# High parts of the weights by a converting DMA instead of staging buffer and ScalarE, and a sixth slot per piece

## The reference

```
layer 1:  nx = rmsnorm(h);  proj = nx @ w_in            # 1024 x 3088
          gated linear attention and dilated attention over proj -> mixed
          h += mixed @ w_out
          h += square(relu(rmsnorm(h) @ w_ff1)) @ w_ff2 # 1024 x 4096, 4096 x 1024
          final rmsnorm
layer 2:  xn = rms_norm(h); proj = xn @ w_in_2          # 1024 x 5632
          stick-breaking attention, HGRN2 recurrence over proj
          mixed = sigmoid(gate_sb) * (o_sb @ w_branch[:512]) + sigmoid(gate_hg) * (o_hg @ w_branch[512:])
          h += mixed @ w_out_2
          h += (silu(hn @ w_gate) * (hn @ w_up)) @ w_down   # inner width 2816
```

## Time and profile before

| | us |
|---|---|
| median of three runs | 1414.1 |
| the profiled execution | 1414.06 |
| its span, first to last instruction | 1412.4 |
| PE busy | 1386.7 (98%) |
| ACT busy | 865.4 (61%) |
| DVE busy | 624.8 (44%) |
| POOL busy | 192.7 (14%) |

### The profile page before, as it was taken

One profiled execution on the slowest core, in us unless ns is written; L12 is line 12 of the kernel. 1 busy time (PEld: TensorE's weight loads), 2 busy tenths in 40 slices (PEclk: granted clock), 3 DMA queues, 4 the chain that ended last, 5 costly groups with the idle time before them and its releaser, 6 DMA issues.

```text
span 1412.4 us, 17525 instructions
## 1 busy us (share of the span) xinstructions
PE 1386.7 (98%) x6784; PEld 1119.7 (79%) x6784; DVE 624.8 (44%) x1216; ACT 865.4 (61%) x1272; POOL 192.7 (14%) x227
## 2 busy tenths in 40 slices
PE   9999999999999999999989999999999999999999
PEld 6977966788888888887867768787788888888887
DVE  6055365521211212357578779954534422341232
ACT  5574566654544535666678778776557645663561
POOL 0210000111111111111100001011111111111110
PEclk9999999999999999999999999999999999999999
DMA  7975544698888888877745556679988888888975
GB/s 227 248 167 131 143 117 97 151 208 194 189 196 196 194 189 199 189 166 170 169 100 119 120 119 163 169 172 269 221 198 186 192 192 200 192 192 194 197 164 125
DMA packets 72791, 248.00 MB, mean 176 GB/s; under 512 B 8098, under 2 KB 8114, under 8 KB 72580
## 3 DMA queue, kind: packets, MB, share of 16 engines
q0 software_dynamic: 31536, 113.54, 47.0%
q1 hardware_dynamic: 40452, 131.73, 28.9%
q10 hardware_dynamic: 720, 1.61, 0.3%
HBM read 240.52 MB, written 6.32 MB: 175 GB/s over the span
## 4 chain that ended last, share of the span: by engine, by line
PE 78%; ACT 8%; DVE 8%; issue 3%; DMA 2%; SPq 0%; DVEq 0%; ACTq 0%
PE bank L466 24%; PE bank L470 24%; PE bank L473 24%; ACT WH L770 2%; ACT WL L778 1%; PE bank L581 1%; PE bank L600 1%; DVE eb L1416 1%; DMA RAW<-in_w_out 1%; PE bank L624 1%; PE bank L614 1%; ACT eb L924 1%; ACT hs L720 1%; DMA gates<-hs 1%; DVE eb L1412 0%
## 5 line engine op out<-in xcount | busy, mean ns | idle before, releaser
L466 PE MATMUL bank<-NH,WH 128*128 128x512 f32 x1152 | 466.4, 406 | 3.5 <-ACT NH L875 1.7
L470 PE MATMUL bank<-NL,WH 128*128 128x512 f32 x1152 | 449.2, 391 | 1.0 <-DVE NL L1160 0.5
L473 PE MATMUL bank<-NH,WL 128*128 128x512 f32 x1152 | 449.3, 391 | 0.0
L770 ACT ACTIVATE WH<-RAW 128x1024 fp32r<-128x1024 f32 (+2 forms) x227 | 235.2, 1037 | 204.8 <-PE bank L473 191.5
L466 PEld LDWEIGHTS bank<-NH,WH 128*128 128x128 f32 x1152 | 216.9, 188 | 69.0 <-issue 26.3
L470 PEld LDWEIGHTS bank<-NL,WH 128*128 128x128 f32 x1152 | 217.0, 188 | 47.8 <-issue 3.8
L473 PEld LDWEIGHTS bank<-NH,WL 128*128 128x128 f32 x1152 | 216.8, 188 | 46.2
L778 ACT ACTIVATE WL<-WH 128x1024 fp32r<-128x1024 f32 (+2 forms) x219 | 229.5, 1048 | 5.6
L470 PE MATMUL bank<-AL,WH 128*128 128x512 f32 x432 | 168.2, 389 | 0.0
L466 PE MATMUL bank<-AH,WH 128*128 128x512 f32 x432 | 168.1, 389 | 0.0
L473 PE MATMUL bank<-AH,WL 128*128 128x512 f32 x432 | 168.0, 389 | 0.0
(11 more groups left out here) (288 smaller groups left out, 1637.7 us busy)
## 6 DMA issues: line engine op xcount, KB each, us to landing
RAW<-in_w_in SPq DMA_DIRECT2D x64, 512.0 KB, 5.5
RAW<-in_w_ff SPq DMA_DIRECT2D x64, 512.0 KB, 6.2
WL<-in_w_ff POOLq DMA_DIRECT2D x64, 512.0 KB, 8.7
WL<-in_w_in POOLq DMA_DIRECT2D x62, 512.0 KB, 7.8
RAW<-in_w_gu SPq DMA_DIRECT2D x44, 512.0 KB, 6.6
WL<-in_w_gu POOLq DMA_DIRECT2D x44, 512.0 KB, 8.8
RAW<-in_w_down SPq DMA_DIRECT2D x20, 512.0 KB, 5.1
WL<-in_w_down POOLq DMA_DIRECT2D x20, 512.0 KB, 8.7
```

The lines of the kernel that those rows point to most:

```text
L466: e.matmul(o, a[0], a[1], start=(k == 0), stop=False)
L470: e.matmul(o, b[0], b[1], start=False, stop=False)
L473: mm = e.matmul(o, c[0], c[1], start=False, stop=(k == t.kt - 1))
L770: e.activation(WH[p % HL][:, 0:n], RAW[p % RAWS][:, 0:n], ACT.Copy).then_inc(*act.sig("high", p))
```

## The change

The RAW buffers and the rounding on ACT stay for the first eight pieces only (RAW now lies where temporaries of a later stage lie). From the ninth piece on POOL issues a DMA that reads float32 from HBM and writes float32r into WH itself (`highs`). It waits, as ACT did, for the last matmul with the slot's former piece. ACT then negates WH into WL, and the adding DMA follows as before. HL is 6 instead of 5. Due times move: the negation is ordered 8.5 instead of 1.5 behind the slot's coming free, the adding DMA 10 instead of 3. SP no longer issues weights after the eighth piece. PE waits for the landing of WH where it waited for ACT.

```diff
-HL = 5
+HL = 6
...
-        RAW = [sb(f"RAW{i}", PIECE) for i in range(RAWS)]
...
         temps = top[0]
+        RAW = [sb(f"RAW{i}", PIECE) for i in range(RAWS)]
+        top[0] = temps
...
-        ADDED = 8
+        ADDED, NEGATED = 8, 8.5
...
+        def high(p):
+
+
+            return ("high" if p < ADDED else f"high_loaded{p % HL}", p)
...
-            if p < 5:
-                return [-20.0, -18.4, -15.4, -13.4, -11.5][p]
+            if p < HL:
+                return [-20.0, -18.4, -15.4, -13.4, -11.5, 4.1][p]
             return plan.used[p - HL] + 0.1

         def low_time(p):
-            return split_time(p) + (3.0 if p >= ADDED else 0.05)
+            return split_time(p) + (NEGATED + 1.5 if p >= ADDED else 0.05)
...
-                        pe.wait_ge(("high", p), hi(x, k0 + k))
+                        pe.wait_ge(high(p), hi(x, k0 + k))
...
             def splits():
-                for p, (u, k, m) in enumerate(plan.pieces):
+                for p, (u, k, m) in enumerate(plan.pieces[:ADDED]):
...
-                        yield split_time(p) + 1.5
+                        yield split_time(p) + NEGATED
                         n = m * plan.units[u][4]
-                        act.wait_ge(("high", p))
+                        act.wait_ge(high(p))
...
+            def highs():
+                for p, (u, k, m) in enumerate(plan.pieces):
+                    if p < ADDED:
+                        continue
+                    yield split_time(p)
+                    st, name, i, kt, cols, k0 = plan.units[u]
+                    src = A[name] if i is None else A[name][i]
+                    u0, j0, m0 = plan.pieces[p - HL]
+                    pool.wait_ge(("product", "block", u0, j0 + m0 - 1))
+                    e.dma_start(WH[p % HL][:, 0:m * cols], src[:, k * cols:(k + m) * cols]).then_inc(
+                        *pool.sig(f"high_loaded{p % HL}", p, by=16))
...
-            yield from merge(zeros(), lows(), masks())
+            yield from merge(zeros(), highs(), lows(), masks())
...
             def weights():
-                for p, (u, k, m) in enumerate(plan.pieces):
+                for p, (u, k, m) in enumerate(plan.pieces[:ADDED]):
```

More of the change, by code:

```diff
@@ L1783, in weights @@
                     if p >= RAWS:
-                        sp.wait_ge(low(p - RAWS) if p - RAWS < ADDED else ("high", p - RAWS))
+                        sp.wait_ge(low(p - RAWS))
                     e.dma_start(RAW[p % RAWS][:, 0:m * cols], src[:, k * cols:(k + m) * cols]).then_inc(
```

## The result

The changed kernel takes 1486.6 us (median of four runs, 1484.1 to 1490.4) against 1414.6 us, a ratio of 1.0514 with a 95% interval of 1.0485 to 1.0542: it is slower, by 72 us, where 56 were forecast.

What follows compares the result with a forecast made beforehand. TensorE was taken to bound the kernel, busy 1386.7 of 1412.4 us. The terms −5.1 − 1 + 58 + 3 = +55 us gave 1470 us; the range for 8 in 10 was 1407 to 1590.

Steps and rivals of the forecast that it cites:

- The circle: Dense stages: loads wait behind adding DMAs, these for negations, these for loads; 11.9 us per unit against TensorE's 10.88, +58 us.
- First adding DMA: First link of the circle: an adding DMA issued into an idle queue lands after 5.8 us, as in quiet.
- The second: Link of the circle: the second adding DMA, behind the first in the queue, takes 2.96 us.
- The rest: Last link of the circle: negation, ACT's start and POOL's issue of the next adding DMA, 1.46 us.
- The order of a queue: Queue q0: assumed to serve its DMAs in order of issue, so loads stand behind adding DMAs; no separate size.
- rival 1: Dense stages: the circle does not bind, only gains and the start's cost remain; 1406 to 1414 us, chance 0.27.
- Rival 3: ACT, held at the negation until the load lands, delivers operand rows late; alone 1415 to 1420 us, chance 0.05.
- The half clock: TensorE's granted clock may fall, beyond the sum, if low parts are late by more than 3 us at once.
- wT and the stretch behind it: Attention: TensorE's waits for ACT's copies into wT shorten as roundings leave ACT, −5.1 us.
- The boundaries: Two stage boundaries: the rounding ahead of the operand rows goes, −1 us.
- The start: Program start: pieces 10 and 12 late without the early load into RAW; +3 us, ends 0 and +7.
- Rival 2: Dense stages: the converting load costs 2.96 us like the adding DMA, 13.2 us per unit; 1564 us, chance 0.16.

Runs made afterwards that it cites:

- pool_later: Changed kernel with only POOL's order moved: each adding DMA due 13.5 instead of 10 cells after its slot comes free; 1408.0 us, ratio 0.9962.
- half_adding: Changed kernel with each adding DMA from the ninth piece on carrying only 64 of the 128 partitions, orders untouched; 1395.3 us, ratio 0.987.
- half_columns: Changed kernel with each converting load from the 21st piece on carrying half of the columns on all 128 partitions; 1435.5 us, ratio 1.0153.
- act_later: Changed kernel with ACT's negations due 12 instead of 8.5 cells after the slot, POOL's order nearly kept; 1492.2 us, ratio 1.0559.
- five_slots: Changed kernel with HL 5 again instead of 6, the rest unchanged; 1483.5 us, ratio 1.0486.

## Why the prediction was right

*The sign and the cause: right.* The circle was forecast at 11.9 us and is 12.1. pool_later takes it away and gains 78.6 us, half_adding shortens it and gains 91, half_columns shortens it by 0.85 us and gains 51, act_later leaves it closed and gains nothing.

*Its terms.* First adding DMA 5.8, measured 5.92: the quiet landing was the right choice, since q1 is silent. The second 2.96, measured 3.41: the term that was too small, taken from q0's share with another queue beside it. The converting load 1.68, measured 1.40. The rest 1.46, measured 1.38. With 1.22 us over TensorE's pace, 74 × 1.22 − 17 = +73 us instead of +58; by stages +30.6 and +44.0 = +74.6 were measured. Against the forecast's +55 the dense blocks are 16.6 us dearer, the boundary at qS 8.0 and the start 2.4, and the attention and recurrence give 8.9 more: 18 us in the sum, where without the last they would be 27. So the total came nearer than its parts by some luck.

*The order of a queue: right.* It was an assumption. The landings at 402.7, 405.7 and 407.1 are in the order of issue. The Trainium skill, *DMA: Bandwidth & Descriptors*, "Queues, rings and completion order", has each engine take a queue's descriptors in ring order; the trace agrees.

*One queue instead of two: free.* pool_later keeps everything in q0 and fills the window of 352 us. The same page, "Issuing engines are not separate DMA queues", says that spreading DMAs over issuing engines saves only issue time, and the trace agrees; but the page's rule led to rival 1's time, and that was wrong: bandwidth was free while the order of issue was not.

*Where it shows: wrong.* I expected "PE <- DMA WL" all through f1 and f2, and a difference of 1 us a unit. Only 4.2 us stand there. ACT, held at the negation, delivers AH late instead (34 us in ten waits), mostly at the first unit of a round of f2 or dn. POOL's turns are 12.1 us long as forecast, TensorE's units are not: they take 10.9 us and now and then 19 to 21. The whole stretch from f1 to qS grew from 351.7 to 382.3 us, where I had said about 380. Rival 3 had this mechanism and I said it decided nothing: right for the time, as five_slots shows, and wrong for the rows to look for.

*The half clock.* I had it as a possible addition beyond the sum. It came, mean clock 0.975 against 0.996 (the place before that matters is that of the earlier trace rows), but five_slots with 0.991 takes nearly the same time. That in a loop that sets the pace TensorE's slower stretches use up waiting that was there anyway is my reading of these two runs, not tested by itself.

*wT and the stretch behind it.* Forecast 8.2 to about 3 us; measured 2.0 in three waits, longest 0.8, and the clock behind it stays at 1.00. The whole stretch from kS to br0 gains 14.0 us where I had 5.1: mis-sized. Every kernel without the roundings gains there, 8 to 14 us. That I counted one kind of wait of TensorE and left ACT's lighter load for all the others is the likely reason; no run separates it.

*The boundaries: wrong sign.* −1 us was forecast. Where f1 begins 2.4 us are gained. But in qS, where I had the circle recover at no cost, the rows NH come late and 7.0 us are lost, part of it at half clock (0.57 in 656 to 664 us):

```profile
PE bank L472 <- ACT NH L939: 3.0, 2, 2.7
```

Between br0 and gu 5.7 us go (a part of the last block's 44.0), and TensorE's waits for AH at the turn from f1 to f2 and from gu to dn are where much of the circle is paid.

*The start: near in size, wrong in place.* +3 forecast, +5.4 at f1. Pieces 10 and 12 were not late (the stages up to qD start 0.3 us earlier). Three adding DMAs and two loads, issued between 55 and 60 us, took up to 11 us to land, ACT waited 9.4 us, VectorE's gX was late, and TensorE lost 6.9 us at 97 us, part of it at half clock.

*Rival 2: wrong.* The converting load costs 1.40 us behind other DMAs, not 2.96.

## What to carry to other kernels

When a change makes an engine that issues DMAs wait, write down who waits for whom until the list comes back to its start, sum the links, and compare with the pace of the engine that bounds: if the loop is longer, the difference is paid on every turn, however idle every engine and queue looks. Then move one issue past another before giving up the change: here the same instructions, 5.5 cells later on two engines, turn +5.1% into −1.0%. Check such a shift at the start of the program too, where slots come free in another rhythm.

## What the runs showed of the hardware

- A converting DMA into a rounded type costs about what a plain one does: 0.18 us a packet of 4 KB, and 1.40 us of the queue for 512 KB, against 1.68 for a plain load with another queue beside it. Issued at 20.5 us of the changed kernel, one landed after 4.1 us, against 3.6 for a plain load in quiet.
- A load onto 64 of the 128 partitions is hardly cheaper than onto all: 0.38 us a packet against 0.18, and the loop stayed at 12.1 us. By columns it halves, 1.40 to 0.64 us. The Trainium skill, *DMA: Bandwidth & Descriptors*, "The descriptor swizzle", has the partitions 0 to 63 behind one half of the ports into SBUF; the doubled packet time agrees with that, and no run here looked at the other half. For the adding DMA, 64 partitions were cheaper, but by far less than half: it landed after 4.3 us instead of 5.9, and a second one 2.8 us behind it instead of 3.4.
- After a wait of TensorE of 3.77 us the granted clock was 0.50 in the next 5.5 us. The 54 us that TensorE of five_slots waits for low parts, in waits of at most 4.4 us and mostly under 2.4, brought little of it: mean clock 0.991.

What stays open: why the second adding DMA takes 3.4 us of the queue and not 2.96, what exactly in the attention and recurrence stages gives 14 us, and why half_columns loses 19.2 us in the last block where its circle explains 6.9.
